# Block 2: index scores and the sparse heads' selection placed between tiles of the input projection

## What is computed

```
rel   = relu(einsum('bqhd,bsd->bqhs', qi, ki))          # 4 heads of 32, qi and ki after rope
score = einsum('bqhs,bqh->bqs', rel, wi) * idx_scale
score = where(s <= t, score, -inf)                      # causal
_, sel = top_k(score, 128)                              # then attention over the selected keys alone
```

## Time and profile before

| | before |
|---|---|
| time, median of 3 runs | 3315.37 us (3315.31 to 3318.84) |
| profiled execution, span from first to last instruction | 3315.3 us |
| mean granted clock of TensorE | 0.987 |
| PE busy | 3209.5 us, 97% |
| PE weight loads busy | 2547.2 us, 77% |
| DVE busy | 1924.1 us, 58% |
| ACT busy | 1440.5 us, 43% |

### The profile page before, as it was taken

One profiled execution on the slowest core, in us unless ns is written; L12 is line 12 of the kernel. 1 busy time (PEld: TensorE's weight loads), 2 busy tenths in 40 slices (PEclk: granted clock), 3 DMA queues, 4 the chain that ended last, 5 costly groups with the idle time before them and its releaser, 6 DMA issues. The chain is left out here.

```text
span 3315.3 us, 51847 instructions
## 1 busy us (share of the span) xinstructions
PE 3209.5 (97%) x20772; PEld 2547.2 (77%) x20772; DVE 1924.1 (58%) x3355; ACT 1440.5 (43%) x2349; POOL 56.8 (2%) x44
## 2 busy tenths in 40 slices
PE   8999999999999999999999999999999999899998
PEld 6777788788877777788888888767678788566786
DVE  6544745677557447446775373268756652478555
ACT  6423523444246225334443243455643443656632
POOL 0010000000000210000000000000000000000000
PEclk9999999999999999999999999999999999999999
DMA  4324332333333224432333253223153442132342
GB/s 164 90 79 145 140 115 77 108 96 98 111 128 92 79 60 164 163 99 89 95 99 111 70 185 113 86 77 86 38 191 116 133 149 102 63 97 59 142 145 70
DMA packets 107694, 358.37 MB, mean 108 GB/s; under 512 B 12681, under 2 KB 13065, under 8 KB 104785
## 3 DMA queue, kind: packets, MB, share of 16 engines
q1 hardware_dynamic: 107472, 355.33, 33.5%
HBM read 310.57 MB, written 38.81 MB: 105 GB/s over the span
## 5 line engine op out<-in xcount | busy, mean ns | idle before, releaser
L224 PE MATMUL banks<-h_high,weights_high 128*128 128x512 f32 x2448 | 980.9, 401 | 16.9 <-DVE weights_low L245 11.7
L225 PE MATMUL banks<-h_low,weights_high 128*128 128x512 f32 x2448 | 956.9, 391 | 0.0
L226 PE MATMUL banks<-h_high,weights_low 128*128 128x512 f32 x2448 | 956.9, 391 | 0.0
L224 PEld LDWEIGHTS banks<-h_high,weights_high 128*128 128x128 f32 x2448 | 461.1, 188 | 125.7 <-DVE weights_low L245 13.4
L226 PEld LDWEIGHTS banks<-h_high,weights_low 128*128 128x128 f32 x2448 | 460.9, 188 | 98.0
L225 PEld LDWEIGHTS banks<-h_low,weights_high 128*128 128x128 f32 x2448 | 461.6, 189 | 93.0 <-issue 3.3
L1854 DVE TENSOR_TENSOR weights_low<-ring,weights_high 128x1024 fp32r<-128x1024 f32 (+2 forms) x124 | 164.6, 1328 | 292.1 <-ACT weights_high L1800 292.0
L1800 ACT CAST weights_high<-ring 128x1024 fp32r<-128x1024 f32 (+2 forms) x124 | 140.6, 1134 | 437.2 <-PE banks L226 437.0
L217 DVE TENSOR_TENSOR weights_low<-ring,weights_high 128x1024 fp32r<-128x1024 f32 x131 | 161.9, 1236 | 277.9 <-ACT weights_high L212 276.5
L212 ACT CAST weights_high<-ring 128x1024 fp32r<-128x1024 f32 x131 | 137.2, 1048 | 378.7 <-PE banks L226 373.6
L1998 ACT CAST weights_high<-ring 128x1024 fp32r<-128x1024 f32 (+1 forms) x116 | 132.5, 1142 | 322.6 <-PE banks L226 322.6
(11 more groups left out here) (473 smaller groups left out, 4902.0 us busy)
## 6 DMA issues: line engine op xcount, KB each, us to landing
ring<-in_in SPq DMA_DIRECT2D x136, 512.0 KB, 4.2
ring<-in_up SPq DMA_DIRECT2D x88, 512.0 KB, 3.6
ring<-in_gates SPq DMA_DIRECT2D x72, 512.0 KB, 4.2
x<-in_gates SPq DMA_DIRECT2D x56, 512.0 KB, 4.2
ring<-in_down SPq DMA_DIRECT2D x32, 704.0 KB, 4.1
ring<-in_out SPq DMA_DIRECT2D x32, 512.0 KB, 3.6
ring<-in_branch SPq DMA_DIRECT2D x16, 768.0 KB, 4.3
stored<-g_spill SPq DMA_DIRECT2D x16, 768.0 KB, 4.5
```

The lines of the kernel that those rows point to most:

```text
L224: pe.matmul(bank, core.wh[:, half, w], high, start=start, stop=False)
L225: pe.matmul(bank, core.wh[:, half, w], low, start=False, stop=False)
L226: return pe.matmul(bank, core.wl[:, half, w], high, start=False, stop=stop)
```

## The change

- The index scores move from `stick_breaking` to `project2`. PE issues the products of query block 3, 2 and 1 in `beside(9)`, `beside(10)` and `beside(11)`, into banks 4, 5, 7 and 6. ACT's relus and DVE's weighting follow in `beside(n)` for n = 10, 11 and 12. PE waits for `ckv_rooted` before the first products, for `rel_out` 4 and 8 before the second and third, and for `rel_out` 12 before the products of `dsa_k` in `beside(12)`.
- The 16 rounds of the selection move from `attention` to DVE's `beside(n)` in `project2`, n = 14 to 31 without 22 and 26.
- `stick_breaking` loses its index products, relus and weighting; a head's logits now wait for the logits of the head before to be taken out (`z_out`).
- The scores and the 8 largest values have a place of their own behind the projection's scratch memory; the relu results lie in the ring behind the weights. SyncE waits for `weighted` 12 before it loads gate weights there at n = 30.

```diff
+INDEX_AT = {9: 3, 10: 2, 11: 1}
+INDEX_ORDER = (3, 2, 1)
+INDEX_END = 13
+RANK_AT = [n for n in range(14, 32) if n not in (22, 26)]
...
@@ project2, sync, n == 30
                     sp.dma_start(w1, b["w1_dram"]).then_inc(sems["w1_landed"], 16)
+                    sp.wait_ge(sems["weighted"], 12)
...
@@ project2, tensor, beside(n)
+                if n in INDEX_AT:
+                    i, turn_n = INDEX_AT[n], INDEX_ORDER.index(INDEX_AT[n])
+                    if turn_n == 0:
+                        pe.wait_ge(sems["turned"], TURNED.index("idx_k") + 1)
+                        pe.wait_ge(sems["sc_out"], 1)
+                        pe.wait_ge(sems["ckv_rooted"], 1)
+                    else:
+                        pe.wait_ge(sems["rel_out"], 4 * turn_n)
+                    for h in range(4):
+                        pe.matmul(banks[rel_banks[h]][:, 0:(i + 1) * P], tile("idx_q")[32 * h:32 * h + 32, i * P:(i + 1) * P],
+                                  tile("idx_k")[32 * h:32 * h + 32, 0:(i + 1) * P], start=True, stop=True).then_inc(sems["rel_mm"], 1)
                 if n == 12:
                     pe.wait_ge(sems["ckv_normed"], 1)
+                    pe.wait_ge(sems["rel_out"], 12)
...
@@ project2, scalar, beside(n), behind n == 11
+                if n - 1 in INDEX_AT:
+                    i, turn_n = INDEX_AT[n - 1], INDEX_ORDER.index(INDEX_AT[n - 1])
+                    for h in range(4):
+                        act.wait_ge(sems["rel_mm"], 4 * turn_n + h + 1)
+                        if turn_n:
+                            act.wait_ge(sems["weighted"], 4 * (turn_n - 1) + h + 1)
+                        act.activation(rel[:, h, 0:(i + 1) * P], banks[rel_banks[h]][:, 0:(i + 1) * P], ACT.Relu)\
+                            .then_inc(sems["rel_out"], 1)
...
@@ project2, vector
+            def weigh(i):
...
+            def rank(r):
+                if r == 0:
+                    own.settle()
+                else:
+                    dve.wait_ge(sems["replaced"], 3 * r)
+                for i in range(1, 4):
+                    dve.max(top[:, i, :], score(i)).then_inc(sems["ranked"], 1)
+                for i in range(1, 4):
+                    dve.wait_ge(sems["ranked"], 3 * r + i)
+                    s = score(i)
+                    dve.match_replace(s, top[:, i, :], s, TAKEN).then_inc(sems["replaced"], 1)
...
@@ project2, vector, beside(n), behind n == 14 and ahead of n == 18
+                if n - 1 in INDEX_AT:
+                    weigh(INDEX_AT[n - 1])
+                if n == INDEX_END:
+                    own(dve.tensor_copy(score(0), causal(0)))
+                if n in RANK_AT:
+                    rank(RANK_AT.index(n))
...
@@ attention, vector
-                if 0 <= d < rounds:
-                    rank(d)
-                    replace(d)
...
@@ stick_breaking, tensor
                 for j in range(4):
-                    if h and j < 3:
-                        pe.wait_ge(sems["rel_out"], 4 * (h - 1) + j + 1)
+                    if h and j == 0:
+                        pe.wait_ge(sems["z_out"], 4 * h)
...
                 if h < 3:
-                    index_products(h + 1)
                     logits(h + 1)
-                    pe.wait_ge(sems["rel_out"], 4 * (h + 1))
...
@@ stick_breaking, scalar and vector
                 if h < 3:
-                    relu(h + 1)
                     logarithm(h + 1)
...
-            own(dve.tensor_copy(score(0), causal(0)))
             softplus(0)
             for h in range(4):
-                if h < 3:
-                    weigh(h + 1)
```

More of the change, by code:

```diff
@@ L2499, in project2, with causal @@
     turned_f, summed_f, ones_f = tmp[0:4, 2, :], tmp[0:4, 3, :], core.root[0:4, :]
+    rel, score, top = core.ring[:, RING * KD * P:RING * KD * P + 4 * T].rearrange("p (h t) -> p h t", h=4), b["score"], b["top"]
+    rel_banks, rounds = (4, 5, 7, 6), SELECTED // 8
+    assert len(RANK_AT) == rounds
+    def causal(i):
+        start = CONST2["causal"] + 384 - i * P
+        return con[:, start:start + (i + 1) * P]
     with phase(nc, *LANDED, "projected", "evacuated", "scaled", "rounded", "split", *NORM, *OPENING, "params", "x_normed", "x_spilled",
@@ L2504, in project2 @@
                "mem_normed", "mk_mm", "mk_out", "mv_mm", "mv_out", "placed", "hid_mm", "hid_parts", "hid_turned", "hid_out", "cmp_mm",
-               "f_biased", "f_exped", "f_logged", "f_turned", "f_scaled", "f_summed", "f_spilled", "own", "own_act", landed=landed) as (block, sems):
+               "f_biased", "f_exped", "f_logged", "f_turned", "f_scaled", "f_summed", "f_spilled", "rel_mm", "rel_out", "weighted",
+               "ranked", "replaced", "own", "own_act", landed=landed) as (block, sems):
         def await_tile(engine, name):
@@ L2815, in _ @@
             own = Own(dve, sems["own"])
+            def weigh(i):
+                done = 4 * INDEX_ORDER.index(i)
+                dve.wait_ge(sems["sc_out"], 1)
+                dve.wait_ge(sems["params"], 16 * len(loads))
+                for h in range(4):
+                    dve.wait_ge(sems["rel_out"], done + h + 1)
+                    wi = b["tm_s"][:, i, IDX_W + h:IDX_W + h + 1]
+                    r = rel[:, h, 0:(i + 1) * P]
+                    if h == 0:
+                        dve.tensor_scalar(score(i), r, wi, None, ALU.mult).then_inc(sems["weighted"], 1)
+                    else:
+                        dve.wait_ge(sems["weighted"], done + h)
+                        dve.scalar_tensor_tensor(out=score(i), in0=r, scalar=wi, in1=score(i), op0=ALU.mult, op1=ALU.add)\
+                            .then_inc(sems["weighted"], 1)
+                dve.wait_ge(sems["weighted"], done + 4)
+                own(dve.scalar_tensor_tensor(out=score(i), in0=score(i), scalar=IDX_SCALE, in1=causal(i), op0=ALU.mult, op1=ALU.add))
+            def rank(r):
+                if r == 0:
+                    own.settle()
+                else:
+                    dve.wait_ge(sems["replaced"], 3 * r)
[5 more added lines that the diff above has]
+                    dve.match_replace(s, top[:, i, :], s, TAKEN).then_inc(sems["replaced"], 1)
+                if r == rounds - 1:
+                    dve.wait_ge(sems["replaced"], 3 * rounds)
+                    for i in range(1, 4):
+                        s = score(i)
+                        own(dve.tensor_scalar(s, s, TAKEN / 2, NEG, ALU.is_gt, ALU.mult))
             def beside(n):
@@ L2921, in attention @@
     around = range(-2, count // 2 + 1)
-    rounds = SELECTED // 8
     assert count % 2 == 0 and all(s % 2 for s in finished)
@@ L2940, in attention @@
     with phase(nc, *EXTRA, "forgotten", "logit_mm", "masked", "exped", "inverted", "ready", "scaled", "t_mm", "t_out", "pv_mm",
-               "y_out", "own", "ranked", "replaced", landed=core.landed[1]) as (block, sems):
+               "y_out", "own", landed=core.landed[1]) as (block, sems):
         @block.sync
@@ L3091, in output @@
                     dve.tensor_tensor(pair(s)["out"], banks[6][:, :], pair(s)["z"], ALU.mult).then_inc(sems["y_out"], 1)
[L3093 to L3110, removed]
             extra_low(dve, sems, core, e, 0)
@@ L3140, in span @@
         return buf[:, h % 2, at[j]:at[j + 1]]
[L3142 to L3148, removed]
+    cum, tails = [(4, 0), (5, 0), (6, 0), (6, 256)], b["tails"]
     def z_bank(j):
@@ L3152, in z_bank @@
         return banks[(0, 1, 2, 1)[j]][:, at:at + width[j]]
-    with phase(nc, *EXTRA, "rel_mm", "rel_out", "weighted", "z_mm", "z_out", "logged", "soft", "tails", "cum_mm", "less", "weights", "pv_mm", "y_out", "own", "own_act") as (block, sems):
+    with phase(nc, *EXTRA, "z_mm", "z_out", "logged", "soft", "tails", "cum_mm", "less", "weights", "pv_mm", "y_out", "own", "own_act") as (block, sems):
         @block.sync
@@ L3171, in _ @@
         def _(pe):
[L3172 to L3179, removed]
             def logits(h):
@@ L3244, in logarithm @@
                 act.activation(whole(soft, h), whole(soft, h), ACT.Ln, bias=core.ones[:, 0:1]).then_inc(sems["logged"], 1)
[L3246 to L3252, removed]
             extra_high(act, sems, core, e, 0)
@@ L3290, in softplus @@
                 own.settle()
[L3292 to L3305, removed]
             extra_low(dve, sems, core, e, 0)
             extra_low(dve, sems, core, e, 1)
-            own.settle()
-            dve.wait_ge(sems["split"], 2)
-            own(dve.tensor_copy(score(0), causal(0)))
             softplus(0)
             for h in range(4):
-                if h < 3:
-                    weigh(h + 1)
                 dve.wait_ge(sems["cum_mm"], h + 1)
@@ L3396, in block2_layer, with score @@
                 loads += ((con[:, :], w["con2"]),)
+            scored = nc.alloc_sbuf_tensor_at(f"score{layer}", [P, 10 * P], F32, offset=next_address(nc))
+            b["top"] = nc.alloc_sbuf_tensor_at(f"top{layer}", [P, 4, 8], F32, offset=next_address(nc) + 4 * 10 * P)
+            def score(i):
```

(6 more changed lines are left out.)

2 lines of the change are left out of this document (1 added, 1 removed).

## The result

The changed kernel takes 3344.88 us (median of 4 runs, 3341.99 to 3345.2), against 3317.11 us for the kernel before in the same comparison (4 runs): 27.8 us more, a ratio of 1.0081 with a 95% interval of 1.0068 to 1.0094. The forecast was 3334 us in a range of 3320 to 3350. The direction and the mechanism were right. (The base was low too, 3315.4 against 3317.1 us in this comparison.

What follows compares the result with a forecast made beforehand. PE alone was taken to set project2's time, with DVE full in attention but not what PE waits for. 53.0 us added less 34.4 removed gave 18.6 more than 3315.3: 3334 us, range 3320 to 3350.

Steps and rivals of the forecast that it cites:

- Four waits for ACT (34.6 us): In project2, PE stands still four times a layer until ACT's square root or last relu: 17.3 us a layer added.
- Table loads: In project2, a table switch costs ACT 1.3 us by the trace; the skill's drains would add 4.1 us a layer.
- Low clock (10.8 us): In project2, PE's clock falls behind the waits: 1.8 us per long wait, half for short, 5.4 a layer added.
- Selection in project2 (2.0 us): DVE's rounds fit in project2, except at n = 19, where the memory's sums become late: 1.0 us a layer added.
- Stick_breaking (17.0 us gained): Without index work in stick_breaking, PE's value products start earlier: 9.5 us gained in the first layer, 7.5 in the second.
- Attention (17.4 us gained): Without the selection in attention, PE's waits of 5.6 and 4.9 us and 6.9 us of low clock go.
- The rival in which DVE's 47 us a layer pay more: DVE paces attention more than PE's waits show: 48 us gained in place of 17.4, 3303 us; chance 0.07.
- The rival of a clock that stays low from wait to wait: In project2, 1.2 GHz persists between the four waits: 18 us a layer in place of 5.4, 3359 us; chance 0.12.
- the sign of being wrong: No PE waits for the relus in project2 (time near 3289 us), or attention shorter by 15 us or more.
- The upper bound of 3350: Range's top: clock price of 3 us a wait and attention's waits only half gone (3334 + 13 + 3).

Runs made afterwards that it cites:

- the filled kernel: Changed kernel with 30, 20 and 11 additional dense products ahead of PE's waits at n = 10, 11 and 12: 3330.19 us, ratio 1.0040.
- the kernel of both edits: Changed kernel with the latent's square root one step earlier and relus and weighting in the step of the products: 3301.08 us, ratio 0.9949.
- The kernels with the order mended: The kernel of both edits, selection's round behind the memory's sums, latent's reciprocal in DVE's step 9: 3291.89 us; also DVE's log sigmoid part in step 11: 3289.39 us.
- the second edit: Changed kernel with ACT's relus and DVE's weighting in the same step as PE's index products: 3299.81 us, ratio 0.9950.

## Why the prediction came out as it did

**Four waits for ACT (34.6 us).** Right: 16.9 us a layer measured, 17.3 forecast. Each wait was within 0.2 us of the path read off the kernel before: 2.3, 7.1, 4.7, 2.8 against 2.1, 6.9, 4.7 and 2.7. The run with the relus in the products' step shows that the order, not the work, makes them.

**Table loads.** In the changed trace, too, the relus follow the log sigmoid at once (it ends at 1981.2, they start at 1981.31). By an estimate from the drain of 1380 ns that the Trainium skill (ScalarE: Activation LUTs, "What ACT_TABLE_LOAD costs") adds to a switch, its two loads would have made the second wait 2.8 us longer; no run here shows it.

**Low clock (10.8 us).** This is the term that was mis-sized. I had taken 1.8 us for a long wait and 0.9 for a short one. Measured are 2.3 to 2.6 for the long ones, 1.7 for the last of each layer, and for the first 1.6 in the first layer and nothing in the second: 14.7 us by the steps. What is left over the waits and products is 8.9 us in the first layer and 7.7 in the second, 16.6 in both; the 1.9 us between the two remain in the filled kernel's steps as well, so they are not low clock; what they are is open. Against 10.8 forecast, 16.6 is 6 of the 7.5 us by which the trace's sum (26.1) exceeds the forecast's (18.6), and 4 of these 6 are low clock. What a wait does to the clock was, and stays, the least certain part: between tiles, 2.3 us lowered it in one layer and not in the other, and 2.2 and 2.1 us in the kernel of both edits did not.

**Selection in project2 (2.0 us).** Right: a wait of 0.9 us a layer (the step is 1.1 us longer), where a round stands ahead of the memory's sums, and nothing else.

**Stick_breaking (17.0 us gained).** 14.2 measured. Head 0 gave more (6.6 us, not 5.0), and then gave it back: "ACT is what limits the rest" was right, but I counted nothing for PE's longer wait at the last exponential and the half clock behind it, 1.7 us in the value products alone. The new wait on `z_out` was free, as I said; another came up that I had not named: PE waits 1.1 us for the gate tile's bank ahead of head 0's products (ACT copies it out only once its exponential and logarithm are done).

**Attention (17.4 us gained).** Somewhat more: 9.9 us in the first layer and 9.8 in the second by the landmarks, 19.7 in all, and 19.8 and 22.0 us of the whole time when the selection's place alone is changed. The rival in which DVE's 47 us a layer pay more falls: DVE went from 82 to 54% busy and PE's share stayed at 97%.

**The rival of a clock that stays low from wait to wait** (3359 us) did not happen: products are back at 0.39 us 3.5 to 5 us after each restart. The last part of the distance, 27.8 us measured against 24.5 between the two profiled spans, is what executions of one kernel differ by: the profiled one of the changed kernel was its fastest, 2.9 us under the median.

**The bounds and the sign of being wrong.** The upper bound of 3350 was added up from 13 us of clock and 3 for attention's waits half gone. Half of the 10.5 us of those waits is 5.3, which would give 3352; the time lies below either. For a kernel in which PE never waits for the relus the prediction named 3289 us. The kernels with the order mended, which also lack the wait for the memory's sums, came out at 3291.9 and 3289.4: the terms other than the stop were about right together.

## What to carry to other kernels

When work is set between the tiles of a phase in which one engine is never idle, look not at how busy the helping engine is but at when its stream reaches the helping part: a consumer that stands one step behind its producer, in a stream that itself waits for the producer's next step, cannot overlap with it. Here ACT was busy 35% of the time and still stopped PE for 17 us a layer; the same relus one step earlier in its stream, ahead of its table loads, stopped PE nowhere. And once a stop is removed, check the engine that was using it to catch up, as here DVE, since the next wait may take its place.

## What the runs showed that was not expected

An idle time of 2.3 us in front of dense products was enough to lower the clock in the first layer, and the low clock already held when PE started again (eight index products took 2.06 us at 1967.92). The same idle time in the second layer left the clock at 1.00 (1.14 us for them), in the changed kernel, in the filled one and in that of the second edit. So the length of a short wait does not tell whether the clock falls; what does is open here. Filling PE's waits with products that nobody needs was worth 14.7 us: the 122 useless products ran where PE stood still, and spared what followed them the low clock.
